# Dilated attention regrouped by token residue: 15 blocks a head in place of 27, and the values summed transposed in one bank

## The reference

```python
DILATION_GROUPS = ((128, 1), (512, 4), (2048, 16))
    span = window // dilation
    qs = to_sub(q).reshape(B, dilation, n_blk, BAND_BLOCK, H, Dh)      # by residue modulo the dilation
    s = jnp.einsum('brnqhd,brnkhd->brnhqk', qs, kb) * (Dh ** -0.5)
    s = jnp.where(valid[None, None, :, None], s, NEG_INF)
    m = jnp.max(s, axis=-1); p = jnp.exp(s - m[..., None]); l = jnp.sum(p, axis=-1)
    ...
    wgt = l * jnp.exp(m - jnp.max(m, axis=0, keepdims=True))           # the three groups of a head are mixed
    o = jnp.sum(wgt[..., None] * o, axis=0) / jnp.sum(wgt, axis=0)[..., None]
```

## Time and profile before

| | us |
|---|---|
| median of 3 runs | 2681.04 (2680.38 to 2682.04) |
| the profiled execution, its own time | 2682.17 |
| its span, first to last instruction | 2680.9 |

### The profile page before, as it was taken

The page is one execution under the profiler, slowest core; times in us unless marked ns, Lnnn a source line. Parts: engine busy times, 40 slices in busy tenths (PEclk is TensorE's granted clock), DMA queues, the critical chain, the costliest instruction groups (busy, mean ns, idle before and its releaser), DMA issues.

```text
span 2680.9 us, 34476 instructions
## 1 busy us (share of the span) xinstructions
PE 2648.4 (99%) x14293; PEld 2180.9 (81%) x14293; DVE 1562.5 (58%) x2811; ACT 1028.2 (38%) x1773; POOL 14.1 (1%) x43
## 2 busy tenths in 40 slices
PE   7999999999999999999999999999999999999999
PEld 5788888889888888766888889888889766888888
DVE  6766444356766456677766636753346677633334
ACT  4652332435322234664422224222234665422223
POOL 1000000000000000000000000000000000000000
PEclk9999999999999999999999999999999999999999
DMA  8255333133555334401555523642224410223321
GB/s 257 79 173 184 113 99 118 64 104 115 202 197 198 111 98 120 139 33 39 182 189 188 204 87 134 208 138 95 94 95 119 142 48 33 79 94 96 108 91 67
DMA packets 298244, 330.58 MB, mean 123 GB/s; under 512 B 13410, under 2 KB 248678, under 8 KB 298088
## 3 DMA queue, kind: packets, MB, share of 16 engines
q1 hardware_dynamic: 297716, 327.83, 37.4%
q10 hardware_dynamic: 372, 0.55, 0.1%
HBM read 319.96 MB, written 2.10 MB: 120 GB/s over the span
## 4 chain that ended last, share of the span: by engine, by line
PE 94%; DVE 4%; ACT 1%; DMA 0%; SPq 0%; issue 0%; DVEq 0%
PE bank L548 27%; PE bank L550 26%; PE bank L549 26%; PE bank L602 2%; PE bank L2437 1%; PE bank L2466 1%; PE bank L576 1%; PE bank L577 1%; PE bank L578 1%; PE bank L1422 1%; PE bank L1412 1%; PE bank L2077 1%; DVE w_lo L516 1%; DMA mw<-in_w_mod 0%; DVE E L2561 0%; PE bank L905 0%
## 5 line engine op out<-in xcount | busy, mean ns | idle before, releaser
L548 PE MATMUL bank<-h_lo,w_hi 128*128 128x512 f32 (+1 forms) x2432 | 914.2, 376 | 3.3 <-DVE h_lo L747 2.2
L550 PE MATMUL bank<-h_hi,w_lo 128*128 128x512 f32 (+1 forms) x2432 | 893.2, 367 | 0.0
L549 PE MATMUL bank<-h_hi,w_hi 128*128 128x512 f32 (+1 forms) x2432 | 892.0, 367 | 0.0
L516 DVE TENSOR_TENSOR w_lo<-raw,w_hi 128x1024 fp32r<-128x1024 f32 (+1 forms) x420 | 489.2, 1201 | 378.8 <-ACT w_hi L510 378.6
L510 ACT ACTIVATE w_hi<-raw 128x1024 fp32r<-128x1024 f32 (+1 forms) x420 | 419.9, 1036 | 339.2 <-PE bank L550 324.2
L548 PEld LDWEIGHTS bank<-h_lo,w_hi 128*128 128x128 f32 x2432 | 458.4, 188 | 88.1 <-issue 8.2
L549 PEld LDWEIGHTS bank<-h_hi,w_hi 128*128 128x128 f32 x2432 | 458.8, 189 | 78.0 <-issue 5.1
L550 PEld LDWEIGHTS bank<-h_hi,w_lo 128*128 128x128 f32 x2432 | 457.7, 188 | 76.3
L548 PE MATMUL bank<-a_lo,w_hi 128*128 128x512 f32 (+1 forms) x1056 | 388.6, 368 | 0.0
L550 PE MATMUL bank<-a_hi,w_lo 128*128 128x512 f32 (+1 forms) x1056 | 384.1, 364 | 0.0
L549 PE MATMUL bank<-a_hi,w_hi 128*128 128x512 f32 (+1 forms) x1056 | 383.8, 363 | 0.0
(11 more groups left out here) (323 smaller groups left out, 2455.0 us busy)
## 6 DMA issues: line engine op xcount, KB each, us to landing
swf<-in_w_ada SPq DMA_DIRECT2D x60, 1024.0 KB, 7.5
raw<-in_ffn_w_gate SPq DMA_DIRECT2D x44, 1024.0 KB, 5.2
raw<-in_ffn_w_up SPq DMA_DIRECT2D x44, 1024.0 KB, 5.2
raw<-in_w_in SPq DMA_DIRECT2D x40, 1024.0 KB, 5.1
raw<-in_ffn_w_down SPq DMA_DIRECT2D x32, 1024.0 KB, 5.2
raw<-in_w_in SPq DMA_DIRECT2D x32, 512.0 KB, 5.2
raw<-in_ffn_w_down SPq DMA_DIRECT2D x16, 768.0 KB, 4.6
mw<-in_w_mod SPq DMA_DIRECT2D x8, 1024.0 KB, 12.0
```

The lines of the kernel that those rows point to most:

```text
L516: nc.vector.tensor_tensor(o, r, half(w_his[place_of[i]], i, h)[0].bitcast(F32), ALU.subtract).then_inc(*w_lo.up((i, h)))
L548: nc.tensor.matmul(o, w1, al, start=start, stop=False)
L549: nc.tensor.matmul(o, w1, ah, start=False, stop=False)
L550: return nc.tensor.matmul(o, w2, ah, start=False, stop=stop)
```

## The change

The queries and keys of the groups of dilation 4 and 16 are stored by token residue modulo 4. Within one residue there are 128 tokens, so each of these groups needs only 4 score blocks, one for each residue (residue r with itself), instead of 10. The group of dilation 1 keeps its 7 blocks (4 on the diagonal, 3 beside it), its queries in a block stored in the order of their residues. That is 15 blocks a head. A score step is now one bank: 128 or 256 columns of the band and 2 x 128 columns of one residue. There are four such steps a head, each with two reductions and two exps (columns up to 256, and the other 256).

A token's softmax now has two parts on different partitions (its row in the band and its row in the residue order), so smallest values and sums are exchanged: VectorE spreads the 16 numbers of a row to 64, TensorE multiplies by a constant matrix (`across`, 64 columns), VectorE gathers, and both parts get a common factor. VectorE multiplies the residue halves of E with it, ScalarE the band halves, before they are transposed. The value products then have the values stationary and the probabilities moving, so the sum for a head comes transposed in one bank and there is no last transpose; the band part takes 256 columns at once where it can. The gate is multiplied with that bank directly, read and written by residue.

Values of the two dilated groups must lie on partitions by residue as well, so for them `natural` loads its stationary operand from every fourth token. The tables in `gm` are 512 columns, not 1280, and E is eight tiles of 512, not two of 1280.

```diff
-    def natural(name, key, t, u, tb2, hook=None):
+    def natural(name, key, t, u, tb2, hook=None, residues=False):
 
         for i in range(2):
-            sl = slice((tb2 * 2 + i) * 128, (tb2 * 2 + i) * 128 + 128)
+            tb = tb2 * 2 + i
+            sl = slice(tb, 512, 4) if residues else slice(tb * 128, tb * 128 + 128)
...
-                    natural(name, key, t, u, m)
+                    natural(name, key, t, u, m, residues=name[2] > 0)
...
-                    nc.scalar.activation(qk2[jh % 2][0][:, g * 512:g * 512 + 512], ps.of(key)[:, :], ACT.Copy).then_inc(
-                        *act.up(("q", jh, g), lets=key))
+                    nc.scalar.activation(att_q(qk2[jh % 2][0][:, g * 512:g * 512 + 512], g), att_from(ps.of(key)[:, :], g),
+                                         ACT.Copy).then_inc(*act.up(("q", jh, g), lets=key))
...
+        def scores(i):
+            t = bank(("as", j, i), A_SC)
+            for g in range(3):
+                pe.wait_ge(act, ("q", j, g))
+                pe.wait_ge(dve, ("k", j, g))
+            lo = 0 if i else 128
+            nc.tensor.matmul(t[:, lo:256], q[:, i * 128:i * 128 + 128], k[:, i * 128 - 128 + lo:i * 128 + 128], start=True,
+                             stop=True)
+            for g in (1, 2):
+                o = g * 512 + i * 128
+                m = nc.tensor.matmul(t[:, 128 + g * 128:256 + g * 128], q[:, o:o + 128], k[:, o:o + 128], start=True, stop=True)
...
+        def across():
+            t = bank(("ax", j), A_AUX)
+            pe.wait_ge(dve, ("ax", j))
+            nc.tensor.matmul(t[:, 0:64], cst["qsum"], amx[:, :], start=True, stop=True).then_inc(*pe.up(("ax", j)))
...
+            if n < 2:
+                for c, (r, g, _) in enumerate(att_blocks(n)):
+                    m = nc.tensor.matmul(ob[:, r * 128:r * 128 + 128], vg[:, g, r, ds], pt[:, c * 128:c * 128 + 128],
+                                         start=(r, g) == (0, 1), stop=True, skip_group_check=True)
+            else:
+                o4 = ob[:, :].rearrange("p (r b i) -> p b r i", r=4, b=4)
+                for kb, c in ((2 * n - 4, 0), (2 * n - 3, 2)):
+                    w = 2 if kb < 3 else 1
+                    m = nc.tensor.matmul(o4[:, kb:kb + w], vg[:, 0, kb, ds],
+                                         pt[:, c * 128:(c + w) * 128].rearrange("p (b r i) -> p b r i", b=w, r=4),
+                                         start=False, stop=True, skip_group_check=True)
...
+        for i in range(4):
+            scores(i)
             yield
         yield
+        across()
         yield
         yield
+        turns(0)
+        yield
+        for n in range(1, 4):
+            turns(n)
+            values(n - 1)
+            yield
+        values(3)
+        yield
```

More of the change, by code:

```diff
@@ L57, in host_constants @@
     res = np.concatenate([c[n] for n in RES], 1)
[L58 to L63, removed]
+    tq = 4 * (p % 32) + p // 32
+    l1 = np.concatenate([m(p[None, :] >= tq[:, None]), m(p[None, :] <= tq[:, None]), m(d >= 0), m((d >= 0) & (d % 4 == 0))], 1)
     def table(n, pos):
@@ L370, in build @@
     vg = here("vv", 3 * 4 * 256)[:, :].rearrange("p (g t n) -> p g t n", g=3, t=4)
-    Es = [here(f"E1_{i}", 1280) for i in range(2)]
-    ot = [sb(f"ot{i}", 512, at=at_a + 8192 + 16384 * i + 6144) for i in range(2)]
+    Es = [here(f"E1_{i}", 512) for i in range(8)]
+    ast, amx, atx = [here(f"ast{i}", 64) for i in range(2)], here("amx", 64), here("atx", 64)
     mg = [sb(f"mg{i}", 512, at=phase1 + 5120 + 2048 * i) for i in range(6)]
@@ L1378, in build @@
     SC = 128.0 ** -0.5
-    GOFF, GW = [0, 256, 768], [256, 512, 512]
-    stat = [small[:, 288 + 16 * i:304 + 16 * i] for i in range(6)]
     ld_gm = sig("gm_in")
[L1382 to L1401, removed]
+    def att_q(t, g):
+        if g:
+            return t.rearrange("p (r q) -> p q r", r=4)
+        return t.rearrange("p (b r i) -> p b i r", b=4, r=4)
+    def att_from(t, g):
+        if g:
+            return t.rearrange("p (q r) -> p q r", r=4)
+        return t.rearrange("p (b i r) -> p b i r", b=4, r=4)
@@ L1403, in pe_att, with att_E, att_blocks @@
+    def att_E(j, i):
+        return Es[j % 2 * 4 + i]
+    def att_blocks(n):
+        if n < 2:
+            return [(r, g, 128 + g * 128) for r in (2 * n, 2 * n + 1) for g in (1, 2)]
+        kbs = (2 * n - 4, 2 * n - 3)
+        return [(kb + o, kb, 128 - 128 * o) for kb in kbs for o in range(2) if kb + o < 4]
     def pe_att(j):
         q, k = qk2[j % 2]
[L1406 to L1440, removed]
+        ds = slice(j % 2 * 128, j % 2 * 128 + 128)
@@ new lines, in across, with turns @@
+        def across():
+            t = bank(("ax", j), A_AUX)
+            pe.wait_ge(dve, ("ax", j))
+            nc.tensor.matmul(t[:, 0:64], cst["qsum"], amx[:, :], start=True, stop=True).then_inc(*pe.up(("ax", j)))
+        def turns(n):
+            t = bank(("at", j, n), A_TR)
+            for c, (i, _, o) in enumerate(att_blocks(n)):
+                pe.wait_ge(dve if n < 2 else act, ("an", j, i))
+                m = turn(t[:, c * 128:c * 128 + 128], att_E(j, i)[:, o:o + 128])
+            m.then_inc(*pe.up(("at", j, n)))
@@ L1441, in pe_att, with values @@
+        def values(n):
+            pt = tmp[(4 * j + n) % 3]
+            pe.wait_ge(*att_copier(j, n))
+            if n == 0:
                 for g in range(3):
@@ L1443, in pe_att @@
                         pe.wait_ge(act if tb2 else dve, ("v", j // 2, g, tb2))
[L1444 to L1455, removed]
@@ L1475, in dve_att @@
[L1475 to L1509, removed]
@@ new lines, in values @@
+                bank(("ob", j), A_OB)
+            ob = ps.of(("ob", j))
+            if n < 2:
+                for c, (r, g, _) in enumerate(att_blocks(n)):
[8 more added lines that the diff above has]
+                                         start=False, stop=True, skip_group_check=True)
@@ new lines, in copy_part @@
+    def copy_part(e, j, n):
+        w = len(att_blocks(n)) * 128
+        e.wait_ge(pe, ("at", j, n))
+        if 4 * j + n >= 3:
+            e.wait_ge(pe, ("av", (4 * j + n - 3) // 4, (4 * j + n - 3) % 4))
+        o, src = tmp[(4 * j + n) % 3][:, 0:w], ps.of(("at", j, n))[:, 0:w]
+        if e is act:
+            nc.scalar.activation(o, src, ACT.Copy).then_inc(*act.up(("ap", j, n), lets=("at", j, n)))
+        else:
+            nc.vector.tensor_copy(o, src).then_inc(*dve.up(("ap", j, n), lets=("at", j, n)))
@@ new lines, in dve_att, with smallest, spread, gathered @@
+    def dve_att(j):
+        st = ast[j % 2]
+        N, L, W, mn, f = st[:, 0:16], st[:, 16:32], st[:, 32:48], st[:, 48:56], st[:, 56:64]
+        quad = cst["quad"]
+        def smallest(i):
+            E, t, lo = att_E(j, i), ps.of(("as", j, i)), 0 if i else 128
+            dve.wait_ge(ld_gm, 0)
+            if j >= 2:
+                dve.wait_ge(pe, ("at", j - 2, 3))
+            dve.wait_ge(pe, ("as", j, i))
+            for a, b, o in ((lo, 256, i), (256, 512, 4 + i)):
+                nc.vector.tensor_tensor_reduce(E[:, a:b], t[:, a:b], gm[:, a:b], -SC, BIG, ALU.add, ALU.min,
+                                               st[:, o:o + 1]).then_inc(
+                                                   *dve.up(("am", j, i, o // 4), lets=("as", j, i) if o > 3 else None))
+        def spread():
+            own = st[:, 0:32].rearrange("p (k o e) -> p k o e", k=2, o=2)[:, :, 0, :]
+            for i in range(4):
+                dve.wait_ge(act, ("ae", j, i))
+            if j:
+                dve.wait_ge(pe, ("ax", j - 1))
+            nc.vector.tensor_tensor(amx[:, :].rearrange("p (k e q) -> p k e q", k=2, q=4),
+                                    own.unsqueeze(3).to_broadcast((128, 2, 8, 4)),
+                                    quad.unsqueeze(1).unsqueeze(1).to_broadcast((128, 2, 8, 4)), ALU.mult).then_inc(
+                                        *dve.up(("ax", j)))
+        def gathered():
+            dve.wait_ge(pe, ("ax", j))
+            nc.vector.tensor_tensor(atx[:, :].rearrange("p (s c q) -> p s c q", s=4, q=4),
+                                    ps.of(("ax", j))[:, 0:64].rearrange("p (s c q) -> p s c q", s=4, q=4),
+                                    quad.unsqueeze(1).unsqueeze(3).to_broadcast((128, 4, 4, 4)), ALU.mult).then_inc(
+                                        *dve.up(("ay", j), lets=("ax", j)))
+            dve.wait_ge(dve, PREV)
+            src = atx[:, :].rearrange("p (k a c q) -> p k a q c", k=2, a=2, q=4)
+            dst = st[:, 0:32].rearrange("p (k o a q) -> p k o a q", k=2, o=2, a=2)
+            for a in range(2):
+                nc.vector.tensor_reduce(dst[:, :, 1, a, :], src[:, :, 1 - a], AX, ALU.add).then_inc(*dve.up(("az", j, a)))
+            dve.wait_ge(dve, PREV)
+            nc.vector.tensor_tensor(mn, N[:, 0:8], N[:, 8:16], ALU.min).then_inc(*dve.up(("amn", j)))
+            dve.wait_ge(dve, PREV)
```

(67 more changed lines are left out.)

52 lines of the change are left out of this document (21 added, 31 removed).

## The result

The changed kernel takes 2692.32 us (median of 4 runs, 2691.76 to 2694.22); the kernel before, on the same chip, 2681.29 us (4 runs). The ratio is 1.0043, with a 95% interval of 1.0031 to 1.0055: slower by 0.4%. The span of the profiled executions grew from 2680.9 to 2691.3 us, at a granted clock of 0.998 in both, so the clock has no part in it.

A forecast was written before the change was run, and what follows sets the result against it. TensorE's issue time, busy 99% of the span, was taken as the bound. 2682.2 - 32.0 (attention) + 39.2 (strided loads) = 2689.4 us, less 1.1 for the profiled execution: 2688 us, range 2647 to 2698 (forecast's own 2678 to 2696).

The forecast's parts named there:

- rival 3: Strided load pays in full and the new attention chain is late: 4 to 12 us more, 2692 to 2700; 0.12 with Rival 4.
- What bounds the kernel: Whole kernel: TensorE, busy 99% of the span; a microsecond of its issue time is one of the end.
- The attention's saving: TensorE in the attention of four heads: 66.4 us before, 8.6 a head after, so 32.0 us saved.
- The strided load: Value units of the dilated groups: 384 weight loads at 0.222 us, not 0.120, so 39.2 us more; range 0 to 46.
- The new chain at nothing: Attention, score steps through `across` to first transposes: covered with 1.2 us left, so costed at nothing.
- Rival 1: Value units of the dilated groups: the strided load costs nothing more, 2649 us; chance 0.27.
- Rival 2: Value units of the dilated groups: strided load paid in part, 0.135 to 0.19 us a matmul; chance 0.11.
- Rival 4: Value products writing their bank in runs of 32 columns: at twice their price 6 us in all; 0.12 with rival 3.
- The break-even: Value units of the dilated groups: matmul distance at which strided loads cancel the attention's saving, 0.203 us.

The follow-up runs named there:

- e1_contiguous: Changed kernel with value units of the dilated groups loading their stationary operand from 128 adjacent tokens again (output differs): 2651.56 us, ratio 0.9887.

## Why the prediction was right

The forecast was 2688 us, the result is 2692.3. It went by the steps that were forecast, and one term was too small. Slower had only a chance of 0.45 there, and 2692.3 also lies at the low end of rival 3's 2692 to 2700; it is the trace, with no late chain and 0.233 us in the value units, that decides for the forecast.

- **What bounds the kernel.** Right. What TensorE issues less or more is in the time nearly one to one: the attention alone took 31.8 us off TensorE's issue time and 29.9 off the median, the strided loads alone added 43.3 and 42.1, each within its interval.
- **The attention's saving, 32.0 us.** Measured 31.8 in the trace (8.5 us a head for the forecast 8.6). The 66.4 us of before was 65.8: the difference belongs to the dense matmuls, which were counted at 0.229 and go at 0.230 there. Its prices, taken from the earlier trace rows, held each; `across` takes 0.23, where 0.22 was taken. The waits inside the score steps went, as said.
- **The strided load, 39.2 us.** The mechanism is as forecast, the size is not: 0.233 us a matmul, not 0.222, so 43.3 us. The price was carried over from VectorE's reading at a step of 32 bytes, as 0.86 ns more an element (the two rows give 0.84 as they stand and 0.90 when the 248 elements are allowed for). The load has its own: 0.45 ns for each word that it spans at steps 3 and 4 (0.173 us for 384 words, 0.233 for 512). That a price of another engine came so near is in part luck: no row before tied the two, and at VectorE's own step of 32 bytes the load takes 0.241. That it has nothing to hide behind was right; TensorE's load unit is busy 56.30 of 56.31 us. This term, 43.3 for 39.2, is the 4 us by which the forecast was low.
- **The new chain at nothing.** Right, with more room than reckoned: VectorE's small operations took 0.17 to 0.22 us each, the four scalings of E halves 1.14 us together, where I had taken 0.43 at most for each of the first two. I gave 1.2 us of reserve; it is about 2.5. The copies of q and k in residue order take 1.1 us where straight ones take 0.6 to 0.7, inside the doubling that I had called covered. Below, the key copy of group 0, straight, and that of group 1 (VectorE, start us, us):

```profile
330.98 0.69 DVE L1703 COPY k_b<-bank 128x512 f32<-128x512 f32 x1 [1.97 <-PE bank L544]
...
343.00 1.09 DVE L1703 COPY k_b<-bank 128x512 f32<-128x512 f32 x1 [2.25 <-PE bank L544]
```

- **Rival 1, the load free: 2649.** Wrong for step 4. The sum for a load that costs nothing more, 2682.2 - 32.0 - 1.1 = 2649, was right: e1_contiguous, with adjacent tokens, takes 2651.6.
- **Rival 2, the load paid in part (0.135 to 0.19 us a matmul).** Wrong at step 4 (0.233); step 3 does it (0.173).
- **Rival 3, a late chain.** Wrong. Even with 2.75 us less to go the turns wait only 0.2 us a head.
- **Rival 4, runs of 32 columns in PSUM.** Wrong. The last band products of a head have 384 columns, 0.64 us at 1.67 ns each; they take 358.11 to 358.68 and the same 0.08 us behind them, 0.65:

```profile
358.11 0.81 PE L1442 MATMUL bank<-tmp,vv 128*128 128x256 f32 x4
358.68 0.48 PE L542 MATMUL bank<-h_lo,w_hi 128*128 128x512 f32 x1
```

- **The break-even,** 0.120 + 32.0 / 384 = 0.203 us a matmul, agrees with the runs: the two medians, at 0.120 and 0.233, lie on either side of before by 29.9 and 11.0 us, and the straight line between them crosses it at 0.120 + 0.113 x 29.9 / 40.9 = 0.203.

## What to carry to other kernels

Before a stationary operand is taken with a step, count the words that its columns span and compare the load with the matmul that it must hide under: here 0.45 ns a word at steps 3 and 4 (at the larger steps 1.7 to 2.1 ns a column), nothing to be seen at 256 words beside 256 moving columns (0.120 us a matmul) and nearly nothing at 512 words beside 512 (0.235 us against 0.229). If it doesn't fit, make the strided side the copy out of PSUM, on an engine that idles, rather than the weight load: that turned a loss of 0.4% into a gain of 1.2%, at the price of 32 transposes more on TensorE, 3.5 us at 0.11 each.

## What the runs showed of the hardware that was not expected

- A weight load's price for a step is not a yes or no: 0.173 us at step 3 lies between 0.120 and 0.234.
- Steps beyond 4 are not all alike: 0.220 at 16 words, 0.241 at 8, 0.266 at 12, each steady through its block of 24 matmuls. Why is open.
- ScalarE and VectorE take longer for a residue order as well: a copy out of PSUM whose neighbouring elements go to places 128 words apart takes 1.1 us for 512 columns on either engine, against 0.6 (ScalarE) and 0.7 (VectorE). Whether the jumps of the write cost this, or the short inner runs of four elements, no run separates.
- The load's price is not that of the moving side: 128 moving columns 4 words apart stay under about 0.12 us, where a load of such columns takes 0.233.
